# A two-block network in fp32 on one core: 512-column dense stages as seven block products, and the memory branch's output gate in the scaling step

## The reference

```python
hl = _modulate(_rmsnorm(xl, norm_g[l, 0]), ml[0], ml[1])
hc = _modulate(_rmsnorm(xc, norm_g[l, 0]), mc[0], mc[1])
ul, uc = _split_cols(hl @ w_in), _split_cols(hc @ w_in)   # q k v o gates | q k v | fourier | 3 merge gates
# memory branch: chunked scan, then
h = _rmsnorm(hf + hb, head_g) * sigmoid(u[3])             # "memory gate" = sigmoid of the projection ml_o
# attention branch: softmax(q1 k1) - lam * softmax(q2 k2), times v, rmsnorm;  Fourier branch: fftn(...).real
y = gm * (ym @ w_br_ml) + gd * (yd @ w_br_da) + gf * (yf @ w_br_fn)     # gm, gd, gf: sigmoids of h @ w_in
x = x + m2 * (y @ w_out)
x = x + m5 * ((silu(a) * b) @ w_ffn_out)                  # a, b = split(modulate(rmsnorm(x)) @ w_ffn_in)
```

## Time and profile before

| | |
|---|---|
| median of three runs | 3517.02 us (3514.33 to 3521.15) |
| span of the profiled execution | 3516.0 us |
| instructions in it | 35829 |
| TensorE busy | 3395.7 us, 97%, 15404 records |
| weight loads busy | 2221.3 us, 63%, 15404 records |
| VectorE busy | 785.6 us, 22% |
| ScalarE busy | 523.7 us, 15% |
| read from HBM | 370.74 MB, 106 GB/s over the span |

### The profile page before, as it was taken

The page is one execution under the profiler, slowest core; times in us unless marked ns, Lnnn a source line. Parts: engine busy times, 40 slices in busy tenths (PEclk is TensorE's granted clock), DMA queues, the critical chain, the costliest instruction groups (busy, mean ns, idle before and its releaser), DMA issues.

```text
span 3516.0 us, 35829 instructions
## 1 busy us (share of the span) xinstructions
PE 3395.7 (97%) x15404; PEld 2221.3 (63%) x15404; DVE 785.6 (22%) x1612; ACT 523.7 (15%) x1043; POOL 0.2 (0%) x4
## 2 busy tenths in 40 slices
PE   8999899999999998999999999999999999999998
PEld 7888588788884454444545444444454785568887
DVE  1012641331012054001830111001020421431101
ACT  1001421130002111001511101000021110321100
POOL 0000000000000000000000000000000000000000
PEclk9999899999999999999999999999999999999999
DMA  5343442334341111322022232111122132133332
GB/s 196 131 168 144 159 155 98 120 145 162 146 170 73 72 48 48 136 79 72 1 108 96 96 120 96 72 72 64 68 101 91 48 120 96 48 132 120 144 128 111
DMA packets 29581, 373.85 MB, mean 106 GB/s; under 512 B 3072, under 2 KB 5248, under 8 KB 5504
## 3 DMA queue, kind: packets, MB, share of 16 engines
q1 hardware_dynamic: 29296, 370.75, 28.4%
q10 hardware_dynamic: 144, 1.05, 0.1%
HBM read 370.74 MB, written 1.05 MB: 106 GB/s over the span
## 4 chain that ended last, share of the span: by engine, by line
PE 92%; DVE 5%; ACT 2%; issue 1%; DMA 0%; SPq 0%; DVEq 0%; ACTq 0%
PE bank L567 91%; DVE small L2330 1%; DVE arena L2304 1%; PE bank L570 1%; ACT arena L1705 0%; DVE arena L2105 0%; DVE arena L1915 0%; ACT arena L1716 0%; DMA masks<-first_consts_dram 0%; DVE arena L2308 0%; DVE arena L1929 0%; DVE arena L2340 0%; DVE h_T L1791 0%; ACT arena L1422 0%; DVE small L2331 0%
## 5 line engine op out<-in xcount | busy, mean ns | idle before, releaser
L567 PE MATMUL bank<-h_T,weights 128*128 128x256 f32 (+1 forms) x5744 | 1702.8, 456 | 19.9 <-ACT masks L1422 5.9
L567 PEld LDWEIGHTS bank<-h_T,weights 128*128 128x128 f32 x5744 | 1089.3, 191 | 604.9 <-issue 499.9
L567 PE MATMUL bank<-arena,weights 128*128 128x256 f32 (+1 forms) x2464 | 705.3, 448 | 20.1 <-DVE arena L2308 11.0
L567 PEld LDWEIGHTS bank<-arena,weights 128*128 128x128 f32 x2464 | 472.8, 192 | 249.2 <-issue 181.7
L567 PE MATMUL bank<-weights,h_T 128*128 128x512 f32 (+1 forms) x768 | 324.0, 583 | 0.0
L567 PEld LDWEIGHTS bank<-weights,h_T 128*128 128x128 f32 x768 | 145.8, 190 | 176.1 <-issue 167.8
L1842 DVE TENSOR_TENSOR arena<-arena,bank 128x256 f32 (+3 forms) x88 | 42.9, 488 | 707.7 <-PE bank L567 707.7
L567 PE MATMUL bank<-arena 64*64 64x64 f32 (+7 forms) x1592 | 184.3, 305 | 16.3 <-ACT arena L1716 8.6
L567 PEld LDWEIGHTS bank<-arena 64*64 64x64 f32 (+2 forms) x1592 | 128.7, 160 | 61.9 <-issue 23.8
L1408 ACT ACTIVATE arena<-bank 128x256 f32<-128x256 f32 (+1 forms) x88 | 38.5, 437 | 664.2 <-PE bank L567 664.2
L567 PE MATMUL bank<-merged_T,weights 128*128 128x256 f32 (+1 forms) x384 | 110.8, 450 | 0.0
(11 more groups left out here) (254 smaller groups left out, 1608.4 us busy)
## 6 DMA issues: line engine op xcount, KB each, us to landing
weights<-wide_slabs_dram SPq DMA_DIRECT2D x151, 2048.0 KB, 7.8
weights<-down_slabs_dram SPq DMA_DIRECT2D x32, 1408.0 KB, 5.8
masks<-second_consts_dram SPq DMA_DIRECT2D x1, 2240.0 KB, 8.5
masks<-second_consts_dram SPq DMA_DIRECT2D x2, 1024.0 KB, 7.1
x_T<-x_T_dram SPq DMA_DIRECT2D x1, 1024.0 KB, 5.8
x_T<-ctx_T_dram SPq DMA_DIRECT2D x1, 1024.0 KB, 11.0
out_dram<-h_T ACTq DMA_DIRECT2D x1, 1024.0 KB, 3.9
masks<-first_consts_dram SPq DMA_DIRECT2D x1, 928.0 KB, 7.4
```

What stands on the lines that cost most here:

```text
L567: return mm(out, lhsT, rhs, start=start, stop=stop, skip_group_check=True)
```

## The change

In layer 0 the dense stages with 512 columns except `ml_o` and `da_gate0`, and in layer 1 `ml_k`, `ml_v`, `da_k`, `da_v`, are computed by Strassen's scheme in Winograd's form. The slab is seen as 2 x 2 blocks (features in two halves of 4 tiles, outputs in two halves of 2), the activations as 2 x 2 (feature halves by x or context). Seven products of such blocks replace eight. One slab (for `ffn_down` two) is a "unit"; units that follow each other form a run (`RUNS`). A product is 8 matmuls of 256 columns (in `ffn_down` 11).

What each engine does for a unit:
- TensorE: products P1, then P4 of the unit before, P2, P5, P6, P3, P7 (`unit_order`). P1, P6, P7 and P4 add up in one bank (0 or 3 in turn), P2 has bank 1, P5 and P3 bank 2.
- VectorE (`block_sum`): four sums of weight blocks of 128 x 1024 (1408 in `ffn_down`), S1 to S4, three of them in place in the ring, S2 in a new tensor `factors`. Per set of activations four sums of 128 x 1024 (`factor_sum`). `join` adds a bank to what ScalarE copied: C11 = P1 + P2, C12 = (P1 + P6) + P3, C22 = P5 + P7's bank.
- ScalarE (`snap`): copies P1, P5 and P6's bank out before the next product adds to the bank. The last corner, C21, is read from the bank after P4 (`corner`, or by VectorE).

Gates, projections and residual additions are applied corner by corner. Slots of the ring come free by the count of products (`used_by`). The norms make the x half of all tiles before the context half. Loops over slabs in these stages are written out. The host lays weight slabs out by blocks; the weights are of the same size.

The memory branch's gate: `L2304` and `L2308` become one instruction per tile, gain times output times `ML_O`. In layer 1, `proj0` waits tile by tile for k of 4 and more (`late`).

The core of the diff (`tt` is tensor_tensor, `ts` tensor_scalar, `stt` scalar_tensor_tensor, `af` an activation):

```diff
+        self.bank = {"P1": x, "P6": x, "P7": x, "P4": x, "P2": 1, "P5": 2, "P3": 2}
...
+def unit_order(key):
+    return ("P5", "P2", "P6", "P3", "P7") if key == ("l0_out", 0) else ("P2", "P5", "P6", "P3", "P7")
...
-                if slab < st.slab0 + st.slabs:
-                    return st.done0 + (slab - st.slab0 + 1) * st.done
+                j = slab - st.slab0
+                if j < st.slabs:
+                    if not in_blocks(st.name):
+                        return "tile_done", st.done0 + (j + 1) * st.done
+                    if (st.name, st.slabs - 1) in UNIT:
+                        return "products", PROD["P4", (st.name, j)]
+                    return "products", PROD["P7" if j % 2 == 0 else "P4", (st.name, j // 2)]
...
+            def product(key, name, ready=None, ks=None):
+                u = UNIT[key]
+                kt = FT // 2 if u.down else 4
+                ks = range(kt) if ks is None else ks
+                if 0 in ks:
+                    if name == "P1":
+                        arrived(u.st, 2 * u.j if u.down else u.j)
+                    if name == "P2" and u.n:
+                        pe.wait_ge(S["joined"], 3 * u.n - 2)
+                    if name == "P5":
+                        if u.n:
+                            pe.wait_ge(S["joined"], 3 * u.n - 1)
+                        pe.wait_ge(S["block_sums"], u.weights("S1"))
+                    if name == "P6":
+                        pe.wait_ge(S["snapped"], u.snap("s1"))
+                        pe.wait_ge(S["block_sums"], u.weights("S2"))
+                    if name == "P3":
+                        pe.wait_ge(S["snapped"], u.snap("s5"))
+                        pe.wait_ge(S["block_sums"], u.weights("S4"))
+                    if name == "P7":
+                        pe.wait_ge(S["snapped"], u.snap("s2"))
+                        pe.wait_ge(S["block_sums"], u.weights("S3"))
+                    if name == "P4":
+                        pe.wait_ge(S["joined"], u.join("C22"))
+                    if u.first and name in ("P5", "P6", "P7", "P4"):
+                        pe.wait_ge(S["factor_sums"], factor_count(factor_set(u.name), ("P5", "P6", "P7", "P4").index(name) + 1))
+                w, b = block_of(u, name), factor_of(u, name)
+                opens = name in ("P1", "P2", "P5")
+                for n in range(1 if u.down else 2):
+                    for k in ks:
+                        if ready and n == 0:
+                            ready(k)
+                        out = bank[u.bank[name]][:, n * T:(n + 1) * T]
+                        if u.tokens:
+                            lhs, rhs = b[:, k, n * P:(n + 1) * P], w[:, k * 256:(k + 1) * 256]
+                        else:
+                            lhs, rhs = w[:, (n * kt + k) * P:(n * kt + k + 1) * P], b[:, k]
+                        last = matmul(out, lhs, rhs, start=opens and n == 0 and k == 0, stop=k == kt - 1)
+                if kt - 1 in ks:
+                    last.then_inc(S["products"], 1)
+            def run_units(keys, before, ready, frees=None):
...
+                    for name in ("P1", "P4", *unit_order(key)):
+                        owner = key
+                        if name == "P4":
+                            if i == 0:
+                                continue
+                            owner = keys[i - 1]
+                        if (owner, name) in before:
+                            before[owner, name]()
...
+            def snap(key, which, scale=1.0):
+                u = UNIT[key]
+                of, into = {"s1": ("P1", "C11"), "s5": ("P5", "C22"), "s2": ("P6", "C12")}[which]
+                act.wait_ge(S["products"], PROD[of, key])
+                if which == "s1" and u.name[3:] in ("da_proj1", "fn_proj1", "out", "ffn_down"):
+                    act.wait_ge(S["block_sums"], u.weights("S1"))
+                af(place(u)[into], bank_of(u, of), ACT.Copy, scale=scale).then_inc(S["snapped"], 1)
...
+            def block_sum(key, which):
+                u = UNIT[key]
+                b, e = blocks(u), spare(u)
+                if which == "S1":
+                    for j in (2 * u.j, 2 * u.j + 1) if u.down else (u.j,):
+                        dve.wait_ge(S[f"landed{u.st.slot(j)}"], u.st.landed(j, 0))
+                    ins = tt(b[2], b[2], b[3], add)
+                elif which == "S2":
+                    if u.n:
+                        before = next(k for k in UNIT if UNIT[k].n == u.n - 1)
+                        dve.wait_ge(S["products"], PROD["P4" if u.first and u.down else "P6", before])
+                    ins = tt(e, b[2], b[0], sub)
+                elif which == "S3":
+                    dve.wait_ge(S["products"], PROD["P1", key])
+                    ins = tt(b[0], b[3], e, sub)
+                else:
+                    dve.wait_ge(S["products"], PROD["P2", key])
+                    ins = tt(b[1], b[1], e, sub)
+                ins.then_inc(S["block_sums"], 1)
+                dve.wait_ge(S["block_sums"], u.weights(which))
+            def sums12(key):
...
+            def join(key, which):
+                u = UNIT[key]
+                of, snapped = {"C11": ("P2", "s1"), "C12": ("P3", "s2"), "C22": ("P7", "s5")}[which]
+                dve.wait_ge(S["snapped"], u.snap(snapped))
+                dve.wait_ge(S["products"], PROD[of, key])
+                dst, src = place(u)[which], bank_of(u, of)
+                ins = stt(dst, src, 1.0 / 16, dst, mul, add) if "ml_k" in u.name else tt(dst, src, dst, add)
+                ins.then_inc(S["joined"], 1)
+                dve.wait_ge(S["joined"], u.join(which))
...
+            def unit(key, take=None, corner=None, inside=None, following=None):
+                block_sum(key, "S3")
+                if corner:
+                    corner()
+                block_sum(key, "S4")
+                for which in ("C11", "C12", "C22"):
+                    join(key, which)
+                    if take:
+                        take(key, which)
+                    if inside and which == "C11":
+                        inside()
+                if following:
+                    sums12(following)
 
...
-                outputs_back(lambda k: pc(p + "ml_g", k))
-                t.wait("act_for_dve")
-                t.out(tt(bT[:, :, 0:nq], bT[:, :, 0:nq], ML_O[:, :, 0:nq], mul), "dve_for_pe")
...
+                    t.out(stt(bT[:, k, 0:nq], bank[4 + k % 4][:, 0:nq], pc(p + "ml_g", k), ML_O[:, k, 0:nq], mul, mul), "dve_for_pe")
```

1020 lines of the change are left out of this document (778 added, 242 removed).

## The result

The changed kernel takes 3344.59 us (median of four runs, 3341.44 to 3347.43), the kernel before, on the same chip, 3519.02 us (3514.33 to 3521.15): a ratio of 0.9507 (0.9493 to 0.952), 174 us less. Forecast were 3351 us with a range of 3335 to 3385; the time is inside it, 6 us under the forecast. The forecast took 166 us off the 3517 us then on record; measured are 174.

The account below looks back on a forecast made before the run. TensorE, busy 97% of a 3516.0 us span, was taken as the bound. Products -164.9, run begins and ends +8.1, gate and hand-offs -8.7 gave 3350.5 us of span; plus 1, forecast 3351 us, range 3335 to 3385.

Parts of the forecast that it names:

- The main term: In converted stages, 5768 narrow records at 217.7 ns replace 3296 wide ones at 431.0 ns, removing 164.9 us.
- The rest of a unit hidden: Inside a run, VectorE's sums and joins and ScalarE's copies stall TensorE nowhere; costed at nothing, tightest margins 2.9 us.
- Run begins and ends: At norms, the ends of out and ffn_down, and attention entries, TensorE waits for others: +8.1 us, bounds 0 and 16.
- The gate and hand-offs: At the memory and attention branches of both layers, shorter waits around the gate: -8.7 us, bounds 0 and -15.
- What I called late next: At layer 0's memory hand-off, C22 and two weight sums (0.7 + 2.5 us) stand ahead of the scaling on VectorE.
- Rival B: Within units, ScalarE's copy or VectorE's sum late once in each: 30 to 60 us, 3381 to 3411; chance 0.08.
- its milder form: Late waits only in gated units and run ends: 10 to 30 us, 3361 to 3381; chance 0.20 together with Rival D.
- Rival C: Weight loads come into the open at 256 columns, slower than before, 3593 at loads of 260 ns; chance 0.03.
- Rival D: Slots held a product longer, loads missed at modulation slabs or before fn: 3356 to 3370; 0.20 with milder Rival B.

Follow-up runs that it names:

- experiment 2: Kernel before with each converted 512-column matmul issued as two of 256: ratio 1.0035; changed kernel with P2 streamed twice in each unit: 0.9996.
- experiment 3: Changed kernel with P4 at its own unit's end: 0.961; with ScalarE's copies of P5 and P6's bank done four times: 0.9526; eight times: 0.9966.
- experiment 4: Changed kernel with sums S1, S3 and S4 over one column: ratio 0.9474; with all four weight sums done twice: 0.956.
- Experiment 1: Kernel before with only the memory gate's part of the change: ratio 0.9979; changed kernel with that part undone: 0.9537.
- experiment 5: Changed kernel with C22, S1, S2 moved behind the scalings at layer 0's branches, and S1, S2 into the root's wait before the feed-forward: 3331.34 us, 0.9468.
- the halved kernel: Kernel before with each 512-column matmul of the converted stages issued as two of 256 columns, all eight products kept: ratio 1.0035.
- the one with eight products: Changed kernel with P2 streamed twice in each unit, all waits and sums kept: ratio 0.9996.
- the kernel with thin sums: Changed kernel with weight sums S1, S3 and S4 over one column instead of 1024 (1408): ratio 0.9474.

## Why the prediction came out right, and what in it was off

- **The main term** (3296 x 431.0 ns against 5768 x 217.7, 164.9 us): the mechanism held, the size was 4.7 us short. Both prices hold the slow start of a stage, once in 1056 records, and so put it on the 5768 narrow records more often than on the 3296 wide ones. At the steady 429.2 and 215.8 ns the products save 169.6 us. The eighth product costs 172 to 177 (824 x 217.7 ns = 179). Halves cost 13 us (8 to 17): the 14.5 of 3296 x 4.4 ns and the 8.2 of the steady distances both fit. Within runs the pace was 215.5 to 216.1 ns, under the 222 at which I would have been wrong. Shown by experiment 2.
- **The rest of a unit hidden**: held. TensorE's waits for VectorE and ScalarE in the converted stages of layer 0 are 13.4 us in sum, or 14.2 with the one before `fn_gate0` that was there before (under 15 forecast), the longest 2.44, none recurring in each unit. Margins as forecast: a copy of four times the length fits, one of eight times doesn't (experiment 3); the sums cost nothing inside ffn_up (experiment 4).
- **Run begins and ends, +8.1 us**: the sum is about right, +7 at the steady prices, and its parts are not. The norm before the feed-forward costs +2.9 (1.4 and a part of the end of out's 2.7 forecast), ffn_up to ffn_down with ffn_down's end +3.2 (1.8 forecast), and each memory scan's entry about 1, which I had at nothing. The norm to `ml_q`, costed at +0.7, gave 1.0 back, and layer 1's norm 1.7. At `ml_q` the rows show the clock: before, 0.61 and 0.54 in the windows from 1058 to 1062, where 16 records took 8.85 us, and 1.00 now. The norms also make the x half of all tiles first now, which is all that P1 needs; that this shortens the norms is read from the order, and no run isolates it.
- **The gate and hand-offs, -8.7 us**: mis-sized the other way, about -13. For the memory branch of layer 0 I had -4.6 at the hand-off, +1.7 for ScalarE being late in the gate's unit and -1.0 of clock, together -3.9. Measured are -3.9 (11.5 to 7.6 us), +0.6 and -2.0, together -5.3. Layer 1's memory branch gave 4.1 and 1.9 of clock, together 6.0 where 3.3 were forecast, without a term for the clock; its attention branch 2.0 (1.3). In layer 0's attention branch the stage with the hand-off costs 0.5 more than its products explain, where 0.2 less was forecast. Experiment 1 gives the gate alone 7 us in the kernel before and 11 in the changed one, but the two intervals overlap. That a separate product would come later still behind C22 and two sums fits the waits (2.4 and 6.5 us); that the two parts of the change help each other isn't shown.
- Together that is -175 instead of -165.5: in spans the forecast was 9.8 us too high (3350.5 against 3340.7), and the three misses point the same way. Of the median it missed 6.4, since the profiled execution stands 3.9 us under the median now and stood 1.0 under it before; these 2.9 us are chance. What I called late next, VectorE's C22 and the next run's sums, was so: experiment 5 moved them and the wait went.
- **Rival B** (30 to 60 us) and its milder form: not there. **Rival C**: out. Loads of 190 ns beside a pace of 215.8 ns on the whole array. The Trainium skill's page "TensorE: Matmul & The Clock Gate", section "The mechanism", says in its list that a load overlaps only where row groups differ; both traces and the halved kernel are against it. The same section also lets a load be pulled ahead when it goes to the background weight buffer, and with that they agree; no run tells the two ways apart. The same page's price for an increment of a semaphore ("The cost: per-tile semaphore tail", given for packed tiles that each increment one) doesn't show in a run: the starts stand 215.8 ns apart with one increment in 16 records (ffn_up), in about 21 (ffn_down) and in about 40 (the feed-forward of the halved kernel). **Rival D**: no wait for weights stands in a converted stage; the slabs land in 7.7 us (7.8 before).

What stays open: the 7 us between the halved kernel and the one with eight products, what the order of the norms' pieces is worth by itself, and how the scheme changes the rounding error, which no run here measures.

## What to carry to other kernels

Where TensorE streams without a gap, seven products for eight give their eighth nearly in full, as long as each copy, sum and join has one whole product (here 3.45 us) between its cause and its use; count the deadline, not VectorE's share. Putting P4 behind the next unit's P1 costs no instruction and was worth 35 us. At the ends of runs the order of VectorE's queue decides: first what frees a bank or feeds the next matmul, then sums for later; it gave as much as leaving out nearly all of three of the four sums.

## What the runs showed of the hardware that I had not expected

- VectorE rewriting the very slab from which TensorE loads costs neither of them anything that these rows show: 928 records in 200 us with VectorE busy 53.5, 79.6 or 118.2 us, and 1225 ns a sum throughout.
- After an idle stretch of 2.44 us in the midst of transposes, which ends at 1360.78, the granted clock is still 1.00 in the window to 1362 and 0.67 and 0.50 in the next two; without that stretch it stays at 1.00. The stop costs about 1 us more than its own length. This isn't certain: five of the traces hold ten such stops of 2.44 us, and no slow clock follows two of them (1799.9 with copies eight times over, 1746.8 in the kernel with the gate undone). None follows the two stops of 1.38 us in the kernel with thin sums.
